# SSD output phase: the diagonal product with its operand roles swapped, on two halves of the array's columns

## The reference, cut to what matters

```
lower_tri = (idx[:, None] >= idx[None, :])
seg = a_cs[:, :, :, None] - a_cs[:, :, None, :]
decay = jnp.exp(jnp.where(lower_tri, seg, -jnp.inf))
scores = jnp.einsum("bcqgn,bcsgn->bcqsg", cmat, bmat)
y_diag = jnp.einsum("bcqsg,bcqsgr,bcsgrp->bcqgrp", scores, decay, xdt)
y_off = jnp.einsum("bcqgn,bcgrpn,bcqgr->bcqgrp", cmat, start_states, jnp.exp(a_cs))
y = (y_diag + y_off)
...
y_l = d_skip * xs_l              # and y of both directions is added to it
...
g = y * jax.nn.silu(z)           # gated_group_rmsnorm begins so
```

## Time and profile before

| what | us |
|---|---|
| median of 3 runs | 3696.69 (3696.56 to 3700.88) |
| the profiled execution's own time | 3691.94 |
| its span in the profile | 3690.1 |
| this phase, first instruction to last DVE result | 2772.4 to 3090.9 |
| one chunk in the steady part, at full TensorE clock | 18.2 |

### The profile page before, as it was taken

How to read it: one execution, slowest core, us unless ns; L and a number is a source line. 1 busy time by engine, 2 the same in 40 slices (tenths; PEclk the granted TensorE clock), 3 DMA queues, 4 the chain that set the end, 5 groups by cost and what they waited for, 6 DMA issues and landing times. The chain is left out here.

```text
span 3690.1 us, 45921 instructions
## 1 busy us (share of the span) xinstructions
PE 3328.2 (90%) x16758; PEld 2694.8 (73%) x16758; DVE 2294.2 (62%) x2782; ACT 1500.1 (41%) x2837; POOL 1996.4 (54%) x1339
## 2 busy tenths in 40 slices
PE   6899999997999999977798998898587997999998
PEld 2777888885788888864797666666466886788886
DVE  5686885225887862227543666676596885667662
ACT  3433223334323223323576554454346663333332
POOL 0487998776869997741000332233268783445442
PEclk8999999998999999998999999999788998999998
DMA  7444333333343333239998555535464555565562
GB/s 260 162 152 144 109 108 121 107 114 126 103 131 121 111 119 110 107 116 355 289 299 253 114 117 124 125 79 130 139 274 164 165 172 197 168 213 190 190 193 100
DMA packets 527747, 587.78 MB, mean 159 GB/s; under 512 B 285739, under 2 KB 406467, under 8 KB 524611
## 3 DMA queue, kind: packets, MB, share of 16 engines
q1 hardware_dynamic: 337197, 401.84, 34.9%
q10 hardware_dynamic: 190328, 183.00, 15.0%
HBM read 381.73 MB, written 203.03 MB: 158 GB/s over the span
## 5 line engine op out<-in xcount | busy, mean ns | idle before, releaser
L751 PE MATMUL pl_bank<-hl_hi,pl_a_hi 128*128 128x512 f32 x2056 | 813.1, 395 | 41.1 <-DVE hl_lo L374 28.2
L753 PE MATMUL pl_bank<-hl_hi,pl_a_lo 128*128 128x512 f32 x2056 | 804.6, 391 | 0.0
L752 PE MATMUL pl_bank<-hl_lo,pl_a_hi 128*128 128x512 f32 x2056 | 804.0, 391 | 0.0
L696 POOL TENSOR_TENSOR pl_a_lo<-pl_sums,pl_a_hi 128x512 fp32r<-128x512 f32 x288 | 437.0, 1529 | 119.6 <-ACT pl_a_hi L800 119.6
L751 PEld LDWEIGHTS pl_bank<-hl_hi,pl_a_hi 128*128 128x128 f32 x2056 | 388.2, 189 | 128.8 <-DVE hl_lo L374 27.6
L753 PEld LDWEIGHTS pl_bank<-hl_hi,pl_a_lo 128*128 128x128 f32 x2056 | 388.3, 189 | 82.1
L752 PEld LDWEIGHTS pl_bank<-hl_lo,pl_a_hi 128*128 128x128 f32 x2056 | 388.9, 189 | 77.9
L800 ACT ACTIVATE pl_a_hi<-pl_sums 128x512 fp32r<-128x512 f32 x288 | 181.8, 633 | 541.9 <-PE pl_bank L753 479.9
L2144 POOL TENSOR_TENSOR mo_w_lo<-mo_w,mo_w_hi 128x1024 fp32r<-128x1024 f32 x96 | 239.4, 2496 | 274.8 <-ACT mo_w_hi L2215 274.6
L696 POOL TENSOR_TENSOR pl_a_lo<-hl_w,pl_a_hi 128x512 fp32r<-128x512 f32 x220 | 309.3, 1420 | 114.6 <-ACT pl_a_hi L800 114.4
L2172 PE MATMUL mo_bank<-mo_hi,mo_w_hi 128*128 128x512 f32 x768 | 305.4, 398 | 21.8 <-POOL mo_w_lo L2144 17.1
(11 more groups left out here) (250 smaller groups left out, 6669.3 us busy)
## 6 DMA issues: line engine op xcount, KB each, us to landing
hl_w<-in_w_rec SPq DMA_DIRECT2D x146, 512.0 KB, 3.5
mo_w<-in_w_br SPq DMA_DIRECT2D x96, 512.0 KB, 4.0
kern_s<-taps_res SPq DMA_DIRECT2D x16, 2048.0 KB, 7.0
spec_xin<-kern_s SPq DMA_DIRECT2D x64, 512.0 KB, 5.5
spec_s<-spec_res ACTq DMA_DIRECT2D x128, 256.0 KB, 4.1
conv_spec<-spec_s SPq DMA_DIRECT2D x240, 128.0 KB, 3.0
g_s<-pl_res ACTq DMA_DIRECT2D x32, 512.0 KB, 2.6
conv_gin<-u_s ACTq DMA_DIRECT2D x32, 512.0 KB, 8.3
```

The costliest lines, as they stand in the source:

```text
L696: nc.gpsimd.tensor_tensor(a_lo[:, at % NS, :], src, a_hi[:, at % NS, :].bitcast(F32), ALU.subtract).then_inc(s_lo, 1)
L751: pe.matmul(out, a_hi[:, q, m], op_hi[:, b, k, :], start=begin, stop=False)
L752: pe.matmul(out, a_hi[:, q, m], op_lo[:, b, k, :], start=False, stop=False)
L753: return pe.matmul(out, a_lo[:, q, m], op_hi[:, b, k, :], start=False, stop=end)
```

## The change

The diagonal product for a head was: `weight` (128 x 128) stationary, `xdt` (128 x 64) moving, result token-major in `p_y`. Now `xdt` is stationary (64 columns) and `weight` moves (128 columns), so that the result is channel-major, with the 64 channels of a head in 64 partitions of PSUM: even heads in partitions 0 to 63, odd heads in 64 to 127, and the loop goes back and forth between the two (`for e in range(2)`, innermost). Two more terms join the same accumulation group: the inputs `x` against `skip` (the identity scaled by `d_row`, made once), and the states part `y` against the identity. The transposes, the DVE additions of skip term and diagonal product, and POOL's product of x and `d_row` are gone. DVE reads the finished bank for the gate, of three `p_y` banks. Chunks are interleaved in halves: on PE two `segments` of chunk c + 1, two `diagonal` of chunk c, two `incoming` of chunk c + 1, twice per chunk. On SP the states are loaded ahead of x, and x waits for the diagonal product of two chunks earlier, as PE now reads it.

```diff
+        skip = ph.sb("skip", [P, HEADS, P])
-        p_y = ph.ps("p_y", [P, 2, 512])
+        p_y = [ph.ps(f"p_y{i}", [P, 512]) for i in range(3)]
-        p_t = ph.ps("p_t", [P, 512])
...
+                sp.dma_start(st[:, q], st_v[c]).then_inc(s_stl[q], 16)
                 if c >= 2:
-                    sp.wait_ge(s_xdt, 3 * c - 3)
+                    sp.wait_ge(s_diag, 4 * c - 4)
                 sp.dma_start(x[:, q, :], x_v[c + NCC, :, 0:D]).then_inc(s_ld[q], 16)
-                sp.dma_start(st[:, q], st_v[c]).then_inc(s_stl[q], 16)
...
-                for n in range(3):
-                    f = ssd["dt"][:, c + NCC, n * HEADS:(n + 1) * HEADS] if n < 2 else ssd["d_row"][:]
+                for n in range(2):
+                    f = ssd["dt"][:, c + NCC, n * HEADS:(n + 1) * HEADS]
...
+            nc.gpsimd.tensor_tensor(skip[:], ssd["ident"][:, None, :].to_broadcast([P, HEADS, P]),
+                                    ssd["d_row"][:, :, None].to_broadcast([P, HEADS, P]), ALU.mult).then_inc(s_skip, 1)
...
             def diagonal(c, b):
+                q, n = c % 2, 2 * c + b // 2
                 pe.wait_ge(s_wt, 8 * c + 2 * b + 2)
                 if b == 0:
-                    pe.wait_ge(s_xdt, 3 * c + 2)
-                    if c:
-                        pe.wait_ge(s_y, c)
-                for h in range(4 * b, 4 * b + 4):
-                    for d in range(2):
-                        mm = pe.matmul(p_y[:, h // 8, (h % 8) * HD:(h % 8 + 1) * HD], weight[:, c % 2, d, h, :],
-                                       xdt[:, c % 2, d, h * HD:(h + 1) * HD], start=(d == 0), stop=(d == 1))
+                    pe.wait_ge(s_xdt, 2 * c + 2)
+                    pe.wait_ge(s_ld[q], 16 * (c // 2) + 16)
+                    pe.wait_ge(s_sum, c + 1)
+                    if c == 0:
+                        pe.wait_ge(s_skip, 1)
+                if b % 2 == 0 and n >= 3:
+                    pe.wait_ge(s_res, n - 2)
+                for i in range(2):
+                    at = slice((2 * (b % 2) + i) * P, (2 * (b % 2) + i + 1) * P)
+                    for term in range(4):
+                        for e in range(2):
+                            h = 4 * b + 2 * i + e
+                            cols = slice(h * HD, (h + 1) * HD)
+                            lhs = (xdt[:, q, 0, cols], xdt[:, q, 1, cols], x[:, q, cols], y[:, q, cols])[term]
+                            rhs = (weight[:, q, 0, h, :], weight[:, q, 1, h, :], skip[:, h, :], ssd["ident"][:])[term]
+                            mm = pe.matmul(p_y[n % 3][e * HD:(e + 1) * HD, at], lhs, rhs, start=(term == 0), stop=(term == 3))
                 mm.then_inc(s_diag, 1)
...
+            for u in range(4):
+                incoming(0, u)
             for c in range(NCH):
-                for u in range(4):
-                    incoming(c, u)
-                for b in range(4):
-                    if c and b < 2:
-                        turn(c - 1, b)
-                    if c + 1 < NCH:
-                        segments(c + 1, b)
-                    diagonal(c, b)
+                for half in range(2):
+                    for b in (2 * half, 2 * half + 1):
+                        if c + 1 < NCH:
+                            segments(c + 1, b)
+                    for b in (2 * half, 2 * half + 1):
+                        diagonal(c, b)
+                    for u in (2 * half, 2 * half + 1):
+                        if c + 1 < NCH:
+                            incoming(c + 1, u)
                 if c + 2 < NCH:
                     scores(c + 2)
...
+            def total(c):
+                dve.wait_ge(s_off, 4 * c + 4)
+                nc.vector.tensor_tensor(y[:, c % 2], y[:, c % 2], off[:], ALU.add).then_inc(s_sum, 1)
...
-                dve.wait_ge(s_turn, 2 * c + b + 1)
+                dve.wait_ge(s_diag, 4 * c + 2 * half + 2)
...
             for c in range(NCH):
-                q = c % 2
-                for u in range(4):
-                    if u == 2 and c:
-                        dve.wait_ge(s_sum, 2 * c - 1)
-                    incoming(c, u)
-                if c:
-                    gated(c - 1, 0)
...
+                for half in range(2):
                     if c + 1 < NCH:
-                        weigh(c + 1, b)
-                dve.wait_ge(s_sum, 2 * c + 2)
-                dve.wait_ge(s_diag, 4 * c + 4)
-                nc.vector.tensor_tensor(y[:, q], y[:, q], p_y[:].rearrange("p a n -> p (a n)"), ALU.add).then_inc(s_y, 1)
+                        weigh(c + 1, 2 * half)
+                        weigh(c + 1, 2 * half + 1)
+                        incoming(c + 1, 2 * half)
+                        incoming(c + 1, 2 * half + 1)
+                    if half and c + 1 < NCH:
+                        total(c + 1)
+                    gated(c, half)
```

More of the change, by code:

```diff
@@ L1765, in phase_ssd_outputs @@
         sc = ph.sb("sc", [P, 2, 2, GROUPS, P])
-        xdt = ph.sb("xdt", [P, 2, 3, D])
+        xdt = ph.sb("xdt", [P, 2, 2, D])
+        skip = ph.sb("skip", [P, HEADS, P])
         off = ph.sb("off", [P, D])
@@ L1771, in phase_ssd_outputs @@
         p_seg = [ph.ps(f"p_seg{i}", [P, 512]) for i in range(2)]
-        p_y = ph.ps("p_y", [P, 2, 512])
+        p_y = [ph.ps(f"p_y{i}", [P, 512]) for i in range(3)]
         p_off = ph.ps("p_off", [P, 2, 512])
-        p_t = ph.ps("p_t", [P, 512])
         s_bc, s_ld, s_stl, s_zl, s_gst = ph.sems("bc_in", 2), ph.sems("ld", 2), ph.sems("stl", 2), ph.sems("zl", 2), ph.sems("gst", 2)
-        s_sp0, s_sp1, s_xdt, s_scm, s_sc = (ph.sem(n) for n in ("sp0", "sp1", "xdt", "scm", "sc_done"))
+        s_skip, s_sp0, s_sp1, s_xdt, s_scm, s_sc = (ph.sem(n) for n in ("skip", "sp0", "sp1", "xdt", "scm", "sc_done"))
         s_seg, s_exp, s_wt, s_diag = (ph.sem(n) for n in ("seg", "exp", "wt", "diag"))
-        s_offm, s_off, s_sum, s_y, s_turn, s_res = (ph.sem(n) for n in ("offm", "off_done", "sum", "ydone", "turn", "res_done"))
+        s_offm, s_off, s_sum, s_res = (ph.sem(n) for n in ("offm", "off_done", "sum", "res_done"))
         bc_v = xbc_s[D:, :].rearrange("(m p) t -> p m t", p=P)
@@ L1820, in inputs @@
                     pool.wait_ge(s_diag, 4 * c - 4)
-                    pool.wait_ge(s_sum, 2 * c - 2)
-                for n in range(3):
-                    f = ssd["dt"][:, c + NCC, n * HEADS:(n + 1) * HEADS] if n < 2 else ssd["d_row"][:]
+                for n in range(2):
+                    f = ssd["dt"][:, c + NCC, n * HEADS:(n + 1) * HEADS]
                     nc.gpsimd.tensor_tensor(heads(xdt[:, c % 2, n, :]), heads(x[:, c % 2, :]),
@@ L1972, in incoming @@
                 if u == 0 and c >= 2:
-                    dve.wait_ge(s_turn, 2 * c - 2)
+                    dve.wait_ge(s_diag, 4 * c - 4)
+                if u == 2 and c:
+                    dve.wait_ge(s_sum, c)
                 nc.vector.tensor_tensor(dst[:, b * 512:(b + 1) * 512].rearrange("p (h n) -> p h n", n=HD),
@@ L1976, in incoming, with gated @@
                                         edge[:, :, None].to_broadcast([P, HEADS // 2, HD]), ALU.mult).then_inc(s_off, 1)
-            def gated(c, b):
+            def total(c):
+                dve.wait_ge(s_off, 4 * c + 4)
+                nc.vector.tensor_tensor(y[:, c % 2], y[:, c % 2], off[:], ALU.add).then_inc(s_sum, 1)
+            def gated(c, half):
                 q = c % 2
-                if b == 0:
+                if half == 0:
                     dve.wait_ge(s_zl[q], 16 * (c // 2) + 16)
@@ L1983, in gated @@
                         dve.wait_ge(s_gst[q], 16 * (c // 2))
-                dve.wait_ge(s_turn, 2 * c + b + 1)
-                nc.vector.tensor_tensor(res[:, q, 4 * b:4 * b + 4, :].rearrange("p m n -> p (m n)"), p_t[:],
-                                        z[:, q, 4 * b:4 * b + 4, :].rearrange("p m n -> p (m n)"),
+                dve.wait_ge(s_diag, 4 * c + 2 * half + 2)
+                nc.vector.tensor_tensor(res[:, q, 4 * half:4 * half + 4, :].rearrange("p m n -> p (m n)"), p_y[(2 * c + half) % 3][:],
+                                        z[:, q, 4 * half:4 * half + 4, :].rearrange("p m n -> p (m n)"),
                                         ALU.mult).then_inc(s_res, 1)
@@ L1992, in _ @@
             scores(1)
+            for u in range(4):
+                incoming(0, u)
+            total(0)
             for c in range(NCH):
-                q = c % 2
-                for u in range(4):
-                    if u == 2 and c:
-                        dve.wait_ge(s_sum, 2 * c - 1)
-                    incoming(c, u)
-                if c:
-                    gated(c - 1, 0)
-                dve.wait_ge(s_off, 4 * c + 4)
-                nc.vector.tensor_tensor(y[:, q], y[:, q], off[:], ALU.add).then_inc(s_sum, 1)
-                dve.wait_ge(s_sum, 2 * c + 1)
-                dve.wait_ge(s_xdt, 3 * c + 3)
-                nc.vector.tensor_tensor(y[:, q], y[:, q], xdt[:, q, 2, :], ALU.add).then_inc(s_sum, 1)
-                for b in range(4):
```

(13 more changed lines are left out.)

10 lines of the change are left out of this document (removed).

## The result

| | us, median | ratio to before, 95% interval |
|---|---|---|
| before | 3698.53 (3696.56 to 3700.88, 4 runs) | |
| changed | 3662.80 (3657.36 to 3667.75, 4 runs) | 0.9903 (0.9885 to 0.9921) |
| changed, again, with later experiments | 3660.92 (3655.20 to 3669.31, 6 runs) | 0.9905 (0.9886 to 0.9924) |

The change is faster by 1.0%, 35.7 us; 3669 us was forecast (27.7 us less), with 3654 to 3691 as the range. The profiled executions differ by 3690.1 - 3655.6 = 34.5 us of span.

What follows compares the result with a forecast made beforehand. Bound: PE's work plus waits for DVE's list. Gains of 24.4 (fourteen intervals, one clock fall) - 0.5 (first pass) + 3.8 (end) = 27.7 us off 3691.9 give 3664.2, plus 4.75 to the median: 3669 us, range 3654 to 3691.

Steps and rivals of the forecast that it cites:

- Pairs at 128 columns: In PE's diagonal product, records of the two column halves run side by side, 0.112 us a pair, 64 pairs 7.2 us.
- rival 1: Diagonal product on PE: no pairs form at 128 columns, it takes 14.3 us a chunk, kernel 3776 us; chance 0.09.
- Rival 2: Diagonal product on PE: weight loads not hidden under matmuls, a pair takes 0.165 us, kernel 3723 us; chance 0.05.
- Waits for the weights and `p_off`: PE's waits for DVE's weights and for the states part to leave `p_off`, 1.5 us per chunk, both go.
- `total`: New PE wait before the first diagonal for DVE's one remaining addition, charged 0.25 us per chunk, 0 to 1.0.
- Sum of PE's work: PE's work per chunk: segments 4.04, diagonal 7.2, scores 0.95, incoming 3.46, shape changes 0.7, together 16.3 us.
- changes of shape: PE's switches of array shape, four per chunk at about 0.17 us each, 0.7 us per chunk.
- Clock: Steady part: one fall of the granted clock taken, between none and two, costing 3.4 us.
- End: End of the phase, after the loop's intervals: 16.1 us becomes 12.3, so 3.8 us less.
- First pass: First pass of the loop: 16.4 us becomes 13.5 plus 3.4 for a clock fall, 16.9, so 0.5 us lost.
- The named signs: Diagonal groups of 64 at 3.6 to 3.8 us, both waits gone, interval 16.3 to 16.9, DVE under 75%, PE over 95%.
- Rival 3: Another PE wait, for `total` or for weights behind ACT's exponentials: interval 17.4 us, kernel 3680 us; chance 0.20.

Runs made afterwards that it cites:

- Experiment 2: The changed kernel with all 32 even-head records of a half chunk listed before all 32 odd-head ones: 3754.38 us, ratio 1.0163.
- Experiment 3: The changed kernel's swapped product with PE and DVE in the order of the kernel before, four incoming groups together: 3723.02 us, ratio 1.0076.
- Experiment 4: The kernel before, product not swapped, with only the change's order of incoming halves and additions: 3749.90 us, ratio 1.0153.
- experiment 5: The changed kernel with DVE additions of 448 columns into an unread buffer behind each chunk's total: five 3738.26 us, three 3711.98 us.
- the first version of 7: The changed kernel with each chunk's diagonal product in one piece on PE: 3699.04 us, ratio 1.0008.
- experiments 1: The changed kernel with each head's four terms issued together, then the next head's: 3681.96 us, ratio 0.9970.
- 6: The changed kernel with a fifth term per head, the states part against the identity once more: 3684.68 us, ratio 0.9972.
- the second version of 7: The changed kernel with the diagonal product in one piece and ACT's small products ahead of the third exponential: 3650.28 us, again 3646.46 us.
- the best version: Another name for the second version of 7: 3650.28 us, ratio 0.9882; again 3646.46 us, ratio 0.9865.

## Why the prediction was right, point by point

- **Pairs at 128 columns.** Taken at 0.112 us from the convolutions, measured 0.109. Experiment 2 shows that the whole result hangs on it: rival 1 gave 3776 for no pairs, the kernel without them took 3754. Rival 2, loads not under the matmuls, would have shown pairs of 0.165. One thing the prediction did not see: the pairs do not need strict alternation, only a record of the other half within four places. The rule of the Trainium skill (TensorE: Matmul & The Clock Gate, "Part 3: Packing small matmuls — row/col tiling") that loads overlap a running matmul only between different row groups does not hold for these fp32 records: all use all rows, each has a load of its own of 0.137 us, and still a pair starts every 0.109.
- **Waits for the weights and `p_off`.** They went, as said. Experiment 3 shows that the gain needs a new order: in the old one the kernel is slower than before. Experiment 4 shows that the order alone does not give it. That the shorter DVE list is needed too is shown only in part: 5.1 us of added work bring the wait for the weights back and undo the gain, but the work taken away was 4.0 us, and that dose was not run.
- **`total`.** Charged 0.25 us per chunk, measured 0.28.
- **Sum of PE's work.** 16.3 forecast, 15.8 measured (16.09 - 0.30). The terms mis-sized: pairs and changes of shape together 7.9 where 3.64 + 3.65 = 7.3 were measured (64 pairs of 0.109 are 7.0, which leaves 0.3 of the 0.7 charged for shapes), and scores at 0.81 for 0.95; segments took 4.2 for 4.04. Over 14 intervals this is most of 231.4 - 224.8 = 6.6 us.
- **Clock.** I charged one fall, 3.4 us, and named PE's idle time as the open point. There was none in the steady part, nor in any kernel with PE full: this term, 3.4 us, did not come. Nor did the fall charged to the first pass, see below.
- **Start and end.** End: -3.8 forecast; from behind the last diagonal of chunk 14 (DVE's addition at 3074.7 before, PE's incoming at 3043.2 now) to the last gate it was 15.4 and is 11.5, -3.9. First pass: +0.5 forecast. It took 14.0 us (2804.4 to 2818.5) where 16.9 was forecast with a fall of the clock in it; the halved stretch ended at 2804.8, as the pass began. With 0.5 us more ahead of the loop the start of the phase comes to -1.8.
- **The sum.** In the phase -1.8 - 34.4 - 3.9 = -40.1 against -27.7, so 12.4 us more gain than forecast: 6.8 by two falls of the clock that did not come, 6.6 by the interval, less 1 elsewhere. The whole kernel shows 35.7, since the phases around this one, with the same code, took 5.7 us more in the profile. That the kernel's time came nearer to the forecast than the phase's did is luck.
- **The named signs.** The groups of 64 took 3.64 us, between 3.6 and 3.8, both waits went, and PE was busy 98%. Two signs were missed: the interval is 16.1 and not 16.3 to 16.9, and DVE is busy 76% and not under 75, with 12.2 us a chunk where 11.7 was forecast.

Rival 3, another wait in place of the old one, is what experiments 3 and 5 and the first version of 7 became. Its conditions are close by: the changed kernel clears them by 2.5 us on DVE (experiment 5) and not at all for `total`, at 0.28 us a chunk.

## What to carry to other kernels

When the engine that is nearly full also waits for one that is not, read how far ahead of its deadline each result of the second engine comes; that room, not the busy share, says what an edit is worth and what may be added. Here DVE was idle 3.9 us of a chunk, its results had 2.5 us of room, and 5.1 us more work cost the whole gain. Swapping roles so that products of 64 columns fill two halves of the array paid here only as long as records of both halves stood within four places of each other in the list. And an idle time that goes can be worth more than its length: in this phase the kernels with PE full had the full clock too.

## What the runs showed of the hardware

- TensorE ran fp32 records of two column halves side by side when they were up to four records apart in its list, and no further. With heads in turn the odd head's first record starts beside the one four places ahead of it (interval 17.37 us); with 32 records of a half in a row only four at the border are paired (21.93 us). A record can so start ahead of earlier ones of the other half: y_weight at 2920.34 stands in the list behind y_skip at 2920.44.
- In the steady part the granted clock was 1.00 in the changed kernel and in experiments 1, 2, 6 and the second version of 7, where PE has no wait over 0.3 us. It fell for 3.4 to 6.8 us at a time, about half of it lost, in the kernel before (longest waits 1.1 and 0.6 us), in experiments 3 to 5 and in the first version of 7 (waits of 1.9 to 4.3 us). At the start of the phase it was halved for a time in the changed kernel too (0.55 from 2801.0 to 2804.8). What brings a fall was not isolated.
- One and the same DVE addition of 1024 columns from SBUF took 1.33 us in the best version, 2.01 in the changed kernel and 3.93 in experiment 4; with POOL idle at its start it took 1.23 (at 3030.22 in the changed kernel). POOL's instruction that ran as the addition began ended at 2899.96, 2902.46 and 2918.40 us, and each addition ended 1.08 us after that, at 2901.04, 2903.54 and 2919.48. So by these rows the addition got through only once that instruction of POOL had ended, and how long it takes goes by where in POOL's instruction it falls. The next one of POOL in the best version took 4.59 us, where its like takes 3.61. The rows are DVE's and POOL's of the changed kernel, then those of the best version:

```profile
2898.85 3.61 POOL L1814 TENSOR_TENSOR y_spread<-ssd_masks,ssd_a_lo 128x2048 fp32r<-128x2048 f32 x1
2901.53 2.01 DVE L1985 TENSOR_TENSOR y_y<-y_y,y_off 128x1024 f32<-128x1024 f32 x1
...
2896.35 3.61 POOL L1814 TENSOR_TENSOR y_spread<-ssd_masks,ssd_a_hi 128x2048 fp32r<-128x2048 f32 x1 [3.49 <-PE y_p_seg L1857]
2899.71 1.33 DVE L1988 TENSOR_TENSOR y_y<-y_y,y_off 128x1024 f32<-128x1024 f32 x1
2899.92 4.59 POOL L1814 TENSOR_TENSOR y_spread<-ssd_masks,ssd_a_lo 128x2048 fp32r<-128x2048 f32 x1
```

So a DVE duration from one order is no constant for another: the three additions of experiment 5 took 5.11 us where 3.8 were expected.
